# Loading the third matrices of a spare quad behind the first matrices of the quad that follows it

## The chip, the core and the metric

The kernel runs on one NeuronCore of a Trainium2 chip. The metric is the device time of one execution in microseconds (us). It computes one inference step of a two-layer backbone for 128 context tokens and 128 sample tokens with width 1024. All of its weights are float32 in HBM and are read once per execution, so the kernel moves some 290 MB.

## The reference, cut to what matters

Each of the two layers has a mixer part (modulated norm, one combined input projection, linear attention, convolution and latent attention, an output projection) and a mixture of experts. The change is in how the weights of the experts are loaded.

```python
def hier_moe(h, p):          # 32 experts in 4 groups; top 1 group, top 2 experts in it, for each token
    ...
    gate = (...)             # (tokens, 32), two entries of a row are not zero
    hid = silu(einsum('bnd,edf->bnef', h, moe_w1)) * einsum('bnd,edf->bnef', h, moe_w3)
    return einsum('bnef,efd->bnd', hid * gate[..., None], moe_w2)
# moe_w1, moe_w3: (2, 32, 1024, 256); moe_w2: (2, 32, 256, 1024): 1 MiB per expert and matrix
```

## The kernel before

**Tiles and quads.** The two routed entries of every token are put into tiles of 32 places (CAP). Each of the 32 experts has one tile of its own. An expert that more than 32 entries chose gets further tiles out of 16 spare ones. Four tiles make a quad: quads 0 to 7 are the base quads (experts 4q to 4q+3), quads 8 to 11 hold the 16 spare tiles. The order in which quads are worked on is written out by hand in ORDER (L88), `[0, 1, 8, 2, 3, 9, 4, 5, 10, 6, 11, 7]`. In what follows i is the position in this order, so the positions 2, 5, 8 and 10 are spare quads and the other eight are base quads. Which spare tiles are in use is known only at run time: SyncE reads four expert numbers with value_load (L668), and a tile that is not in use has the number 32 (NE).

**Matrices and buffers.** A quad has three matrices for each tile, of 1 MiB each. The first and second ones (moe_w1 and moe_w3) are the eight "up" matrices of a quad, and the third ones (moe_w2) its four "down" matrices. Half p=0 of a quad (tiles 0 and 1) is loaded into ring_b, half p=1 (tiles 2 and 3) into ring; in both, the slots 0 to 3 take up matrices and the slots 4 and 5 down matrices. So each half has one buffer for up matrices and one for down matrices, and there is no second buffer for the next quad. All these loads are issued by SyncE (L639 and L651) and go through one queue, q1.

**What the loads wait for.** up_weights(i, 0) waits until TensorE is done with the up matmuls of half 0 of position i-1 (L631, up_psum 2i-1). up_weights(i, 1) waits for the same of half 1 (L625 and L626). down_weights(i, 0) and (i, 1) wait until both halves of the down matmuls of i-1 are done (L643, down_psum 2i). SyncE works on its instructions in order, so an issue that waits holds every issue behind it. The order is: up 0, up 1, down 0, down 1 of i, and then those of i+1.

**Predicated loads.** The loads of a spare quad have a condition (L619): where the expert number is 32, the transfer is skipped. Its semaphore still gets its 16, and what was in the buffer stays there; the gate rows of an unused tile are zero places, so that its matmuls add nothing. TensorE works through a spare quad in full whether its tiles are used or not.

**TensorE's order** (L1420 to L1448) is also written out. For each position i: up(i) (L1394) unless i is spare; a gather of tokens for the next pair of quads (L1376); combine(i-1) (L1405), which adds the outputs of the quad before into the result; another gather; the transposes of hid (L1433); then, **if i+1 is spare, up(i+1)**; and last down(i) (L1445), which waits for the down matrices of i (L1438). So the up matmuls of a spare quad come just before the down matmuls of the quad ahead of it.

ScalarE does silu on the up results (L944) and copies hidT (L954) and y_hi (L959), VectorE forms hid (L1861) and y_lo (L1881).

Of the kernel before, what the change touches and what calls it, by code (L numbers as in the profile page):

```python
# [95 lines left out]
def spare(i):  # L96

    return i < QUADS and ORDER[i] >= BASE_QUADS
# [96 lines left out]
def build(nc, a, o):  # L195

    ctx = ExitStack()
    with ctx:
# [328 lines left out]
        def vectors(lay):  # L527

            def rows(r0, n, src):
                return vecA[r0:r0 + n, :], src.rearrange("(r p) -> r p", p=P)  # L530

            return [rows(r0, n, a[name][lay]) for r0, n, name in (
                (R_ADA, 48, "ada_b"), (R_N1, 8, "norm1_w"), (R_N2, 8, "norm2_w"), (R_GLA, 2, "gla_norm_w"), (R_CB, 2, "conv_b"),
                (R_CW, 2, "conv_ln_w"), (R_CLB, 2, "conv_ln_b"), (R_QN, 2, "mla_qnorm_w"), (R_KVN, 1, "mla_kvnorm_w"))] + [
                rows(R_FIN, 8, a["final_norm_w"]),
                (vecB[0:2 * CONV_K, :], a["conv_w"][lay].rearrange("k (t p) -> (k t) p", p=P))]
# [27 lines left out]
        def _(sp):  # L564
# [11 lines left out]
            for l in range(L):  # L576
# [37 lines left out]
                def source(name, i, x, held):  # L614

                    q = ORDER[i]
                    if q < BASE_QUADS:
                        return a[name][l, 4 * q + x], {}
                    return a[name][l, sp.snap(held[x] % NE)], {"cond": held[x] < NE}  # L619

                def ring_free(i, slot, freed):
                    if i == 0:
                        last = max(g for g in range(units(l)) if g % RING == slot)
                        sp.wait_ge(*unit_done.at(l, last + 1))
                    elif slot in (0, 4):  # L625
                        sp.wait_ge(*freed)  # L626

                def up_weights(i, p, held=None):

                    if p == 0 and i > 0:  # L630
                        sp.wait_ge(*up_psum.at(l, 2 * i - 1))  # L631
                    for g in range(4):
                        src, skip = source(("moe_w3", "moe_w1")[(g // 2) ^ p], i, 2 * p + g % 2, held)
                        if p == 0:
                            into, landed = ring_b, ring_b_up_landed
                        else:
                            ring_free(i, g, up_psum.at(l, 2 * i))
                            into, landed = ring, ring_landed[g]
                        sp.dma_start(into[:, g, :], src.rearrange("(p k) n -> p (k n)", k=KT), **skip).then_inc(landed, 16)  # L639

                def down_weights(i, p, held=None):
                    if p == 0 and i > 0:
                        sp.wait_ge(*down_psum.at(l, 2 * i))  # L643
                    for x in range(2):
                        src, skip = source("moe_w2", i, 2 * p + x, held)
                        if p == 0:
                            into, landed = ring_b, ring_b_down_landed
                        else:
                            ring_free(i, 4 + x, down_psum.at(l, 2 * i))
                            into, landed = ring, ring_landed[4 + x]  # L650
                        sp.dma_start(into[:, 4 + x, :], src.rearrange("(p k) n -> p (k n)", k=2), **skip).then_inc(landed, 16)  # L651
# [9 lines left out]
                up_weights(0, 1)  # L661
                down_weights(0, 1)
                sp.wait_ge(*eid_ready.at(l, 1))
                for i in range(1, QUADS):
                    held = None
                    if spare(i):
                        v = 4 * (ORDER[i] - BASE_QUADS)
                        held = [sp.value_load(eid[0:1, v + x:v + x + 1], min_val=0, max_val=NE) for x in range(4)]  # L668
                    up_weights(i, 0, held)
                    up_weights(i, 1, held)  # L670
                    down_weights(i, 0, held)
                    down_weights(i, 1, held)
                    if i == 1 and l + 1 < L:
                        for dst, src in vectors(l + 1):
                            sp.dma_start(dst, src).then_inc(vec_landed.sem, 16)
# [1239 lines left out]
```

## Time and profile before

| | |
|---|---|
| median of 3 runs | 1065.86 us (1064.49 to 1067.51) |
| the profiled execution, its own time | 1068.25 us |
| its span, first to last instruction | 1066.2 us |
| mean granted TensorE clock | 0.874 of full speed |
| TensorE matmul / VectorE / ScalarE busy | 796.1 (75%) / 434.5 (41%) / 260.1 us (24%) |
| queue q1 (all loads by SyncE) | 284.39 MB, 67.8% of 16 engines' span |
| SyncE's down loads waiting for TensorE's down matmuls (L651 for L1445) | 199.0 us, 22 times |
| SyncE's up loads waiting for up matmuls (L639 for L1394) | 175.6 us, 26 times |

The experts of layer 0 take about 252 to 554 us of the span, those of layer 1 about 770 to 1048 us. "DMA share" is the mean busy share of the 16 DMA engines, "PEclk" the granted clock of TensorE as a part of full speed. The duration of a load's row at SyncE is the time that its issue takes, not the transfer. A row of the timeline merges several instructions ("x4"); matmuls overlap, so the end of the last one is later than the start of the next group.

### The profile page before, as it was taken

The page shows a single profiled execution, that of the slowest core. Times are in us where ns is not written, and L with a number is a line of the kernel's source. Part 1 is how long each engine was busy: PE and PEld are TensorE (multiplying, and loading weights), DVE is VectorE, ACT ScalarE, POOL GpSimd, SP SyncE. Part 2 cuts the span into 40 slices and gives each one's busy share as a digit, 9 for nine tenths or more (in the row PEclk, how much of TensorE's full clock was granted, in tenths as well). Part 3 has the DMA queues.
Part 4 walks back from the last instruction along what each step waited for, and adds up shares of the span by engine and source line. Part 5 has one row for each costly group of instructions (what it writes and reads, how often), then busy time and mean ns, then how long its engine had stood idle before and what let it go on. Part 6 is the DMA issues. An engine that isn't in the chain of part 4 may idle for free.

```text
span 1066.2 us, 17503 instructions
## 1 busy us (share of the span) xinstructions
PE 796.1 (75%) x7505; PEld 536.6 (50%) x7505; DVE 434.5 (41%) x934; ACT 260.1 (24%) x488; POOL 36.3 (3%) x52
## 2 busy tenths in 40 slices
PE   4599899958664595687767998988668667576856
PEld 3388566835332363254345974677435334353524
DVE  1348985264211222141225798834714113122214
ACT  2356144132010110020115731533212001101103
POOL 4000100000300000000000001000000000000000
PEclk9699999968678898798888998998789889889968
DMA  9945746955949949948693486347094995977491
GB/s 339 334 140 207 288 161 234 401 238 205 408 157 424 420 178 424 420 171 342 273 367 100 159 311 245 116 179 302 10 423 187 421 381 234 421 292 313 183 424 68
DMA packets 73289, 290.51 MB, mean 272 GB/s; under 512 B 8650, under 2 KB 33948, under 8 KB 47868
## 3 DMA queue, kind: packets, MB, share of 16 engines
q1 hardware_dynamic: 69174, 284.39, 67.8%
q0 software_dynamic: 1504, 3.45, 1.0%
q10 hardware_dynamic: 2534, 1.56, 0.5%
q8 instruction: 59, 0.97, 0.4%
q14 instruction: 18, 0.15, 0.0%
HBM read 382.28 MB, written 1.47 MB: 360 GB/s over the span
## 4 chain that ended last, share of the span: by engine, by line
PE 39%; DMA 36%; DVE 13%; ACT 4%; SPq 4%; issue 2%; ACTq 0%; DVEq 0%
DMA ring<-in_moe_w 27%; PE bank L1394 13%; PE bank L1060 5%; PE bank L1445 4%; PE bank L1294 3%; DVE acc L1638 3%; SPq L639 3%; DMA ada<-in_ada_w 3%; DMA ring_b<-in_moe_w 3%; PE bank L1376 2%; DMA ring<-in_ada_w 2%; PE bank L1003 2%; PE bank L1405 1%; DMA ring<-in_w_in 1%; PE bank L1336 1%
## 5 line engine op out<-in xcount | busy, mean ns | idle before, releaser
L1861 DVE SCALAR_TENSOR_TENSOR hid<-sil,gs,bank 64x256 f32<-64x256 f32 x48 | 32.5, 676 | 323.2 <-ACT sil L944 323.2
L944 ACT ACTIVATE sil<-bank 64x256 f32<-64x256 f32 x48 | 18.1, 378 | 363.9 <-PE bank L1394 363.9
L1394 PE MATMUL bank<-ring_b,hT 128*32 128x256 f32 x768 | 60.4, 483 | 60.4 <-DMA ring_b<-in_moe_w 58.6
L1445 PE MATMUL bank<-ring_b,hidT 128*32 128x512 f32 x384 | 88.6, 603 | 12.7 <-ACT hidT L954 6.2
L1394 PE MATMUL bank<-ring,hT 128*32 128x256 f32 x768 | 60.2, 481 | 40.4 <-DMA ring<-in_moe_w 40.4
L1445 PE MATMUL bank<-ring,hidT 128*32 128x512 f32 x384 | 88.5, 603 | 0.0
L1394 PEld LDWEIGHTS bank<-ring_b,hT 128*32 128x32 f32 x768 | 31.0, 138 | 92.3 <-issue 44.0
L1394 PE MATMUL bank<-ring,xn 128*32 128x256 f32 x768 | 55.5, 452 | 28.4 <-DMA ring<-in_moe_w 28.4
L1394 PE MATMUL bank<-ring_b,xn 128*32 128x256 f32 x768 | 55.0, 450 | 26.2 <-DMA ring_b<-in_moe_w 24.7
L1394 PEld LDWEIGHTS bank<-ring,hT 128*32 128x32 f32 x768 | 34.8, 137 | 65.0 <-issue 58.2
L1638 DVE SCALAR_TENSOR_TENSOR acc<-zp,convT,acc 128x256 f32<-128x256 f32 x120 | 61.8, 556 | 1.9
L1376 PE MATMUL bank<-S,h_hi 128*128 128x256 f32 x192 | 52.7, 308 | 10.0 <-DVE y_lo L1881 8.6
L1294 PE MATMUL bank<-mixT,ring 128*128 128x256 f32 x256 | 56.9, 381 | 2.9 <-DVE mixT L1708 1.8
L1394 PEld LDWEIGHTS bank<-ring,xn 128*32 128x32 f32 x768 | 31.7, 130 | 50.9 <-issue 41.9
L1060 PE MATMUL bank<-x_hi,win_hi 128*128 128x256 f32 x192 | 55.4, 288 | 2.1 <-DVE win_lo L1534 2.1
L1394 PEld LDWEIGHTS bank<-ring_b,xn 128*32 128x32 f32 x768 | 29.7, 129 | 52.9 <-issue 27.5
L1881 DVE TENSOR_TENSOR y_lo<-bank,y_hi 128x512 fp32r<-128x512 f32 x48 | 32.8, 691 | 53.2 <-ACT y_hi L959 53.1
L1060 PE MATMUL bank<-x_lo,win_hi 128*128 128x256 f32 x192 | 54.3, 283 | 0.0
L1060 PE MATMUL bank<-x_hi,win_lo 128*128 128x256 f32 x192 | 54.3, 283 | 0.0
L1445 PEld LDWEIGHTS bank<-ring_b,hidT 128*32 128x32 f32 x384 | 23.0, 111 | 60.6 <-issue 49.0
L1294 PEld LDWEIGHTS bank<-mixT,ring 128*128 128x128 f32 x256 | 48.1, 190 | 10.5 <-DVE mixT L1708 2.6
L1376 PEld LDWEIGHTS bank<-S,h_hi 128*128 128x128 f32 x192 | 37.7, 197 | 22.7 <-DVE y_lo L1881 14.1
(342 smaller groups left out, 1471.3 us busy)
## 6 DMA issues: line engine op xcount, KB each, us to landing
ring_b<-in_moe_w SPq DMA_DIRECT2D x144, 1024.0 KB
ring<-in_moe_w SPq DMA_DIRECT2D x144, 1024.0 KB
ring<-in_ada_w SPq DMA_DIRECT2D x40, 1024.0 KB
ring<-in_w_in SPq DMA_DIRECT2D x14, 1024.0 KB
ada<-in_ada_w SPq DMA_DIRECT2D x4, 2048.0 KB, 23.7
ring<-in_w_out SPq DMA_DIRECT2D x8, 1024.0 KB
wuq<-in_mla_wuq POOLq DMA_DIRECT2D x2, 768.0 KB, 9.5
ring<-in_w_in SPq DMA_DIRECT2D x2, 640.0 KB
```

What stands on the lines that cost most here:

```text
L639: sp.dma_start(into[:, g, :], src.rearrange("(p k) n -> p (k n)", k=KT), **skip).then_inc(landed, 16)
L944: act.activation(sil[64 * p:64 * p + 64, :], B[4 + 3 * p][64 - 64 * p:128 - 64 * p, 0:256], ACT.Silu).then_inc(sil_ready.sem, 1)
L1003: ins = pe.matmul(bank[CM * t:CM * t + CM, 0:256], condS[:, k, :], w[:, k % 2, t * 256:t * 256 + 256], start=(k == 0), stop=(k == KT - 1))
L1060: ins = pe.matmul(out, weights, moving, start=(k == 0 and j == 0), stop=(k == KT - 1 and j == 2))
L1294: ins = pe.matmul(B[WOUT_BANKS[u]][:, f * T:f * T + T], w[:, k, f * P:f * P + P], mixT[:, k, :], start=(k == 4), stop=(k == 1))
L1336: ins = pe.matmul(B[5 + s][:, 0:NG + NE], hT[:, k, s * N:s * N + N], wr[:, k, :], start=(k == 0), stop=(k == KT - 1))
L1376: ins = pe.matmul(bank[:, (k % 2) * BCOLS:(k % 2) * BCOLS + BCOLS], h_part[:, s, k, :], S[:, s, :], start=(s == 0 and h_part is h_hi), sto ...
L1394: ins = pe.matmul(B[4 + 3 * p][CAP * g:CAP * g + CAP, 0:256], tokens[:, k, c:c + CAP], w[:, g, k * 256:k * 256 + 256], start=(k == 0), sto ...
L1445: ins = pe.matmul(B[5 + half][CAP * x:CAP * x + CAP, :], hidT[:, m, CAP * x:CAP * x + CAP], w[:, 4 + x % 2, m * D + half * 512:m * D + hal ...
L1638: ins = dve.scalar_tensor_tensor(acc[:, m, :, :], src, w, acc[:, m, :, :], ALU.mult, ALU.add)
L1861: dve.scalar_tensor_tensor(hid[rows_, i % 2, :].rearrange("s (m p) -> s p m", m=2), sil[rows_, :].rearrange("s (p m) -> s p m", m=2), gs[r ...
L1881: dve.tensor_tensor(y_lo[:, 512 * half:512 * half + 512], B[5 + half][:, :], y_hi[:, 512 * half:512 * half + 512].bitcast(F32), ALU.subtra ...
```

## The change

Before, SyncE issues the down loads of every position right behind its up loads. After, the down loads of a spare position i-1 are left out at i-1 and issued at the next position i, which is always a base quad (two spare quads never follow each other, and the last position is a base quad): behind up_weights(i, 0) and up_weights(i, 1), and ahead of down_weights(i, 0). Their waits and their conditions are the same, and the four register values with the expert numbers are kept for one more position (held_before). Nothing else is changed: no load is added or taken away, and the programs of the other engines are the same.

```diff
                 sp.wait_ge(*eid_ready.at(l, 1))
+                held_before = None
                 for i in range(1, QUADS):
                     held = None
                     if spare(i):
...
                     up_weights(i, 0, held)
                     up_weights(i, 1, held)
-                    down_weights(i, 0, held)
-                    down_weights(i, 1, held)
+
+                    for late in ([i - 1] if spare(i - 1) else []) + ([] if spare(i) else [i]):
+                        down_weights(late, 0, held_before if late < i else None)
+                        down_weights(late, 1, held_before if late < i else None)
+                    held_before = held
                     if i == 1 and l + 1 < L:
                         for dst, src in vectors(l + 1):
                             sp.dma_start(dst, src).then_inc(vec_landed.sem, 16)
```

| | order of SyncE's loads around a spare position 5 |
|---|---|
| before | up 5, **down 5**, up 6, down 6 |
| after | up 5, up 6, **down 5**, down 6 |

## Rows read from the trace of the kernel before

**Rows 1.** The page's chain of waits: shares of the span by engine and line.
```profile
PE 39%; DMA 36%; DVE 13%; ACT 4%; SPq 4%; issue 2%; ACTq 0%; DVEq 0%
DMA ring<-in_moe_w 27%; PE bank L1394 13%; PE bank L1060 5%; PE bank L1445 4%; PE bank L1294 3%; DVE acc L1638 3%; SPq L639 3%; DMA ada<-in_ada_w 3%; DMA ring_b<-in_moe_w 3%; PE bank L1376 2%; DMA ring<-in_ada_w 2%; PE bank L1003 2%; PE ban
```
**Rows 2.** The chain in order of time, layer 0, positions 4 to 6 (start, us, what).
```profile
349.54 22.84 DMA ring<-in_moe_w
372.62 6.03 PE bank L1394 x64
...
382.88 7.04 PE bank L1394 x128
389.92 3.48 PE bank L1445 x32
...
397.67 20.18 DMA ring<-in_moe_w
418.10 5.53 PE bank L1394 x64
```
**Rows 3.** Timeline of SyncE's queue: start, us, line, transfer, count.
```profile
393.41 0.24 SPq L651 DMA_DIRECT2D ring_b<-in_moe_w  x2
...
394.04 2.05 SPq L639 DMA_DIRECT2D ring_b<-in_moe_w  x4
...
403.20 0.81 SPq L651 DMA_DIRECT2D ring_b<-in_moe_w  x2
...
410.37 2.88 SPq L639 DMA_DIRECT2D ring_b<-in_moe_w  x4
```
**Rows 4.** Windows: busy PE, PEld, DVE, ACT, POOL; PEclk, DMA share, GB/s.
```profile
381.50:393.40 11.90, 11.85 (x172) 6.23 (x170) 4.65 (x11) 1.74 (x4) 0.00 (x0) 1.00 0.01 2
397.00:455.00 58.00, 35.69 (x382) 19.90 (x381) 12.36 (x32) 5.26 (x11) 0.00 (x0) 0.82 1.01 422
393.40:397.00 3.60, 2.21 (x18) 2.21 (x19) 0.69 (x1) 1.19 (x2) 0.00 (x0) 1.00 0.51 146
```
**Rows 5.** Timeline of TensorE, position 5: up in two halves, a gather, the first down matmuls.
```profile
382.81 3.66 PE L1394 MATMUL bank<-ring_b,xn 128*32 128x256 f32 x64
386.28 3.64 PE L1394 MATMUL bank<-ring,xn 128*32 128x256 f32 x64
...
394.79 0.39 PE L1376 MATMUL bank<-S,h_hi 128*128 128x256 f32 x1 [1.44 <-DVE y_lo L1881]
...
399.50 0.62 PE L1445 MATMUL bank<-ring_b,hidT 128*32 128x512 f32 x2 [0.47 <-ACT hidT L954]
```
**Rows 6.** DMA queues, 772 to 804 us, layer 1: packets and bytes.
```profile
DMA packets 1720, 12.53 MB, mean 391 GB/s; under 512 B 192, under 2 KB 192, under 8 KB 192
```
**Rows 7.** SyncE's skipped up loads: timeline of two groups, issue time (ns, min/median/max) of another.
```profile
789.43 0.98 SPq L639 DMA_DIRECT2D ring_b<-in_moe_w  x4
800.09 0.96 SPq L639 DMA_DIRECT2D ring<-in_moe_w  x4
```
```profile
L639 SPq DMA_DIRECT2D ring<-in_moe_w x4: 73/76/92, 283.0 to 283.8; - x4
```
**Rows 8.** The last of seven such places, layer 1, positions 10 and 11: SyncE and TensorE.
```profile
1009.94 1.92 SPq L639 DMA_DIRECT2D ring_b<-in_moe_w  x4
```
```profile
998.72 3.66 PE L1394 MATMUL bank<-ring_b,hT 128*32 128x256 f32 x64 [0.61 <-issue]
```
**Rows 9.** Layer 0, positions 2 and 3: timelines of SyncE and TensorE.
```profile
313.88 0.82 SPq L651 DMA_DIRECT2D ring_b<-in_moe_w  x2
```
```profile
300.88 6.06 PE L1394 MATMUL bank<-ring_b,hT 128*32 128x256 f32 x64 [14.06 <-DMA ring_b<-in_moe_w]
...
321.31 0.62 PE L1445 MATMUL bank<-ring_b,hidT 128*32 128x512 f32 x2 [1.75 <-issue]
```
**Rows 10.** Down matmuls behind a long idle time of TensorE, from the chain.
```profile
521.97 26.16 DMA ring<-in_moe_w
...
548.26 5.29 PE bank L1445 x32
```

## The prediction

> **What bounds the kernel now.** I read the chain of waits first, then its stretch inside the experts, then the timelines of SyncE and TensorE and the DMA shares of the same stretch. The chain's largest line is the wait for expert matrices in ring, 27% of the span, with 3% for ring_b; the up matmuls follow with 13% [rows 1]. In order of time a pattern repeats: a transfer ends, up matmuls run, and near a spare position a stretch of pure TensorE work stands in the chain, after which a transfer has to start from nothing [rows 2]. For positions 4 to 6 of layer 0, the up matrices of half 1 of position 4 arrive, TensorE does that half (6.03 us), gathers and combines, does up(5) (7.04 us, both halves) and down(4) (3.48 us), and only then does SyncE issue up(6), at 394.04 [rows 2, 3]. The DMA share shows what this costs: 0.01 from 381.5 to 393.4, then 1.01 at 422 GB/s for the next 58 us [rows 4]. So the expert part is bound by the one load queue, and it has a hole ahead of each base quad that follows a spare one. The hole is there because the order of issue puts down(5), which waits for TensorE's down(4), ahead of up(6), which waits only for up(5).
>
> **The places.** There are eight spare positions, four in each layer. The issue times tell which are empty. Two skipped down loads take 0.24 us at SyncE, two real ones 0.81 [rows 3]. At position 2 of layer 0 the first pair takes 0.82: two spare tiles are in use there [rows 9]. At the other seven positions the pairs look like the empty one. So seven places carry next to no bytes, and one carries two real third matrices.
>
> **An empty place, step by step.** Up(6), half 0, waits for up(5), half 0. Its matmuls start at 382.81 and last 3.66 us, so they end at 386.47 [rows 5]; SyncE follows 0.02 us later, at 386.49. Before, the issue was at 394.04 [rows 3]. Gain: 394.04 - 386.49 = 7.55 us. Half 1 is issued from about 389.9, when up(5) half 1 is done (386.28 + 3.64) [rows 5]; half 0 alone keeps the engines busy for 4.19 MB / 422 GB/s = 9.9 us, so that makes no hole. At the last of the seven: 1009.94 - (998.72 + 3.66 + 0.02) = 7.54 us [rows 8]. The five between give 7.54 or 7.55 in the same way.
>
> Does the whole stream move with it? Four things could be late.
>
> First, TensorE's down(5): it waits for the skipped loads, which SyncE now issues behind up(6). SyncE is done with up(6) at about 392 and waits for down(4) until 393.4 as before. The skip is over by 394, and TensorE needs it at 399.50 [rows 5], provided that a skipped load gives its 16 at once. Between 772 and 804 us the queues moved 12.53 MB, that is 12 real loads of 1.05 MB, with 192 packets under 512 B, exactly 16 for each real load [rows 6]. Eight skipped loads were issued in that stretch [rows 7] and left none. A skipped load takes 73 to 92 ns at its issue [rows 7]. So its 16 do not come through the queue, and I take them as immediate: cost 0.
>
> The Trainium skill, "DMA: Bandwidth & Descriptors", section "Why a DMA increments its semaphore by 16 and not by 1", says that engines that take no part in a transfer have their increments written by the issuing sequencer without waiting. Read for a transfer in which none takes part, this agrees with the packet count.
>
> Second, down(6): it still waits for down(5), and is issued at 403.20 [rows 3]. A transfer gets going 1.7 us behind its first issue: 146 GB/s over 3.6 us is 0.53 MB, worth 1.25 us at 422, so up(6) counts from 395.75 [rows 4]. After the change up(6) runs from 386.49 + 1.7 = 388.2 to 408.1 (8.39 MB, 19.9 us), and down(6) is ready to flow at 404.9. Spare time: 3.2 us; cost 0. If this cover went, each microsecond past it would be lost once.
>
> Third, up(7) half 0 waits for up(6) half 0 on TensorE. Its data are through at 388.2 + 9.9 = 398.1, so TensorE goes straight on from down(5), whose end released the issue at 403.20, and is done 3.66 us later, at 406.9, against an issue at 410.37 before [rows 3]; the stream needs it at 418. Fourth, everything further on is released by the landings themselves, which all move by 7.5 us. So cost 0 for both, and the next spare position starts with its whole chain moved.
>
> Seven places: 7 x 7.54 = 52.8 us.
>
> **The place with two real matrices** (layer 0, position 2). Up(3) can go at 300.88 + 6.06 + 0.02 = 306.96, where before it stood behind the down loads of 313.88 [rows 9]. But now 8.39 MB go ahead of the 2.10 MB that TensorE needs for down(2), and TensorE does down(2) before up(3). Stream: 308.7 + 10.49 MB / 422 GB/s = 333.5; landed 0.7 us later (as down(2) before: flowing from 313.88 + 1.7, 5.0 us of data, used at 321.31 [rows 9]) or up to 2.2 (as up(6), whose data were through at 415.6 and were used from 418.10 with 0.25 of that for issue [rows 2]). TensorE has then been idle for over 14 us (from 321.31 - 1.75 [rows 9]), and the down matmuls take 5.29 us as behind the long wait of [rows 10], instead of 3.48. Down(3) is issued at 339.5 to 341.0 and flows from 341.2 to 342.7. Before, the same bytes (down 2 and up 3) were through at 315.6 + 24.9 = 340.5. So the early start is given back in a new hole: a loss of 0.7 to 2.2 us. At the fast price of down it would be a gain of 0.9. I take +1.5, since the long idle time is certain, and keep -0.9 and +2.2 as ends.
>
> **The sum.** -52.8 + 1.5 = -51.3 us on the profiled execution's own 1068.25, so 1016.95. That execution is 2.39 us above the median of the runs (1065.86). Forecast: 1014.6 us. Unknown sizes of 0.5 us at each of seven places, the ends above and the 1.6 us by which runs differ give the likeliest case 1009 to 1021.
>
> **Rivals.**
> *The skipped loads wait their turn* (ends slower). Place: TensorE's wait ahead of down(5). If the 16 of a skipped load came only when all that was issued before it has landed, down(5) would wait for up(6), half 1. Its landing came 23.8 us behind the first issue (417.85 - 394.04) [rows 2, 3], now 386.49 + 23.8 = 410.3. Down(5) then takes 5.29 us at the low clock, down(6) is issued at 415.6 and flows from 417.3, against 415.6 before: 1.7 us lost at each of seven places instead of 7.5 gained. 1068.25 + 11.9 + 1.5 = 1081.7, or 1079 on the median. It decides from the point where down(5) starts later than about 408.6. The 192 packets speak against it [rows 6]; for it speaks only that no row has TensorE waiting for a skipped load with a full queue ahead. Chance 0.07.
>
> The Trainium skill, same page, section "Queues, rings and completion order", says that an engine takes its descriptors in ring order and that a semaphore's increment lands only after that engine's earlier writes. By that rule a skip that went through the rings would behave like this rival; real matrices, as those of layer 0, position 2, do by either.
>
> *The hole opens again ahead of down(6).* Gather, combine, transposes and down(5) take TensorE from 394.79 to the issue at 403.20, at full clock where the window shows it [rows 3 to 5]. If they ran at half clock, they would take up to 8.3 us more; 3.2 are covered, 5.1 lost, and 2.4 stay of each 7.5: 7 x 2.4 - 1.5 = 15.3, so 1053 us, or 1051 on the median. Against it: TensorE is not idle ahead of this stretch, before or after the change, and PEclk is 1.00 in the window [rows 4]. A smaller share of it is more likely than all. Chance 0.09.
>
> *The issue does not move*, because something else holds SyncE or the queue is already full. Against it: the queue is empty from 381.5, and SyncE's only wait there is down(4)'s. Time 1066, chance 0.04.
>
> *The forecast*: 0.80.
>
> **How the numbers follow.** About 0.3%, 3.2 us, is what a measurement of this kernel can tell from no change. Faster: 0.80 + 0.09 = 0.89. Same: 0.04. Slower: 0.07. The range starts a little under the likeliest case, at 1006, and goes up to 1038, to take in smaller shares of the second rival.
>
> **What would show it right or wrong.** Right: SyncE's first load behind each empty spare up is issued while TensorE's down matmuls of the quad ahead start, not 0.6 us behind their end; the 12 to 14 us with a DMA share near 0 shrink to about 4.5 to 6.5; no idle time of TensorE appears ahead of down at positions 5, 8 and 10; position 2 of layer 0 has a wait of some 14 us ahead of down(2) and a short hole behind it, and stands where it stood by position 4; the other stretches keep their lengths. Wrong: TensorE waits for a transfer ahead of down(5), or a hole in the DMA share between up(6) and down(6).

## The result, and the profile after

| | before | after | ratio, 95% interval |
|---|---|---|---|
| first comparison (4 runs each) | 1066.68 us median | 1025.2 us (1018.67 to 1026.62) | 0.9588 (0.9527 to 0.9649) |
| second comparison, another chip (11 and 6 runs) | 1072.75 us | 1021.97 us (1017.2 to 1026.96) | 0.9517 (0.9490 to 0.9544) |
| forecast | 1065.86 us | 1014.6 us | 0.952 |

The profiled execution after took 1026.62 us (span 1024.6 us, mean granted clock 0.879), 41.6 us less of span than the one before. The kernel moved the same 284.39 MB on q1; the share of the span rose from 67.8% to 70.7%.

SyncE's queue after, at the place of [rows 3]: start, us, line, transfer, count. L639 are up loads, L651 down loads.

```profile
390.49 2.15 SPq L639 DMA_DIRECT2D ring_b<-in_moe_w  x4
393.94 1.76 SPq L639 DMA_DIRECT2D ring<-in_moe_w  x4
397.38 0.28 SPq L651 DMA_DIRECT2D ring_b<-in_moe_w  x2
397.75 0.24 SPq L651 DMA_DIRECT2D ring<-in_moe_w  x2
407.19 0.82 SPq L651 DMA_DIRECT2D ring_b<-in_moe_w  x2
```

TensorE after, at the place of [rows 5] (the up matmuls are now L1398, the down matmuls L1449):

```profile
386.77 3.66 PE L1398 MATMUL bank<-ring_b,xn 128*32 128x256 f32 x64
390.25 3.64 PE L1398 MATMUL bank<-ring,xn 128*32 128x256 f32 x64
...
403.49 0.62 PE L1449 MATMUL bank<-ring_b,hidT 128*32 128x512 f32 x2 [0.47 <-ACT hidT L958]
...
406.94 3.64 PE L1398 MATMUL bank<-ring_b,hT 128*32 128x256 f32 x64
...
414.57 5.28 PE L1398 MATMUL bank<-ring,hT 128*32 128x256 f32 x64 [3.99 <-DMA ring<-in_moe_w]
```

Up(5) half 0 ends at 386.77 + 3.66 = 390.43, and up(6) is issued at 390.49, where before it came 7.57 us behind that point (394.04 against 386.47). The four skipped loads of down(5) go out at 397.38 to 398.0, while up(6) still flows: its half 1 lands only at about 414.2. TensorE does not wait for that. It starts down(5) at 403.49, held only by ScalarE's copy, as in [rows 5]. It then goes straight into up(6) half 0 with no idle time, at 406.94.

The DMA shares there, to set beside [rows 4] (columns as there):

```profile
384.50:391.50 7.00, 7.00 (x109) 4.99 (x111) 3.08 (x9) 0.77 (x2) 0.00 (x0) 1.00 0.14 50
390.50:394.00 3.50, 3.50 (x68) 2.04 (x64) 0.68 (x1) 0.43 (x2) 0.00 (x0) 1.00 0.68 225
394.00:409.00 15.00, 13.08 (x138) 7.14 (x134) 7.79 (x21) 3.70 (x7) 0.00 (x0) 1.00 1.02 425
394.00:451.00 57.00, 40.20 (x432) 22.74 (x425) 14.45 (x35) 7.55 (x16) 0.00 (x0) 0.88 1.01 422
```

The hole is 6.4 us long instead of 14.8 (one minus the DMA share, summed over 384 to 394 us after and over 380 to 397 us before), and the stream behind it has no second one: share 1.02 through 409, where down(6), issued at 407.19, has to take over, and 1.01 at 422 GB/s over 57 us.

Position 2 of layer 0, the one with two real third matrices, to set beside [rows 9]: SyncE first, then TensorE.

```profile
309.79 2.02 SPq L639 DMA_DIRECT2D ring_b<-in_moe_w  x4
313.24 1.76 SPq L639 DMA_DIRECT2D ring<-in_moe_w  x4
316.68 0.82 SPq L651 DMA_DIRECT2D ring_b<-in_moe_w  x2
317.59 0.26 SPq L651 DMA_DIRECT2D ring<-in_moe_w  x2
343.65 0.82 SPq L651 DMA_DIRECT2D ring_b<-in_moe_w  x2
```
```profile
337.17 1.07 PE L1449 MATMUL bank<-ring_b,hidT 128*32 128x512 f32 x2 [14.81 <-issue]
```

Down(2) waits 14.81 us, because its 2.1 MB flow behind the 8.4 MB of up(3); the profile names no releaser for this wait, and experiment 3 tests the reason. Down(3) is issued at 343.65, and from 335.5 to 345.1 the DMA share is 0.20:

```profile
335.50:345.10 9.60, 7.93 (x64) 2.78 (x68) 1.38 (x2) 1.20 (x2) 0.00 (x0) 0.62 0.20 48
```

**Step by step.** The table gives the time from the first load of one up group to that of the next, from the timelines of SyncE. A spare position lies in each of the first four steps (2, 5, 8 and 10); the last column is from the issue of up(11) to the end of down(11).

| profile | layer | up(1)→up(3) | →up(6) | →up(9) | →up(11) | →end |
|---|---|---|---|---|---|---|
| before | 0 | 63.16 | 78.93 | 75.81 | 44.43 | 39.2 |
| after | 0 | 55.47 | 80.70 | 67.67 | 37.72 | 39.4 |
| after, second profile | 0 | 55.34 | 80.87 | 67.71 | 37.49 | 39.2 |
| before | 1 | 44.87 | 74.31 | 74.90 | 45.09 | 37.4 |
| after | 1 | 37.54 | 67.08 | 68.50 | 37.87 | 42.3 |
| after, second profile | 1 | 40.41 | 67.71 | 68.73 | 37.76 | 40.0 |

Layer 0 lost 20.6 us from up(1) on, layer 1 23.2; 2.4 were added ahead of the experts of layer 0, where nothing was changed (up(1) issued at 254.32, before at 251.95). 20.6 + 23.2 - 2.4 = 41.4 of the 41.6.

A step also holds the landing of a whole quad, so it varies by more than the change does. The stretch on which the change acts is shorter: from the first load of the spare quad's half 1 (issued when TensorE is done with half 1 of the up matmuls ahead) to the first load of the next up group. At position 5 of layer 0 it was 379.03 to 394.04, 15.01 us, and is now 383.04 to 390.49, 7.45 us. At the seven empty places it took 14.93 to 15.64 us before and 7.42 to 8.18 us in the first profile after: 7.43 to 7.56 us less at each, where 7.54 or 7.55 was forecast. The second profile after gives the same range, 7.43 to 7.55.

### The profile page after: what moved, and what is told of

Its sections match the earlier page's. It is cut to its first block, busy times and chain, and to the rows that moved or that the text cites. A ratio compares the mean times of both kernels' runs of the same rounds, so it can differ in the third digit from the quotient of the medians.

```text
span 1024.6 us, 17503 instructions
## 1 busy us (share of the span) xinstructions
PE 781.9 (76%) x7505; PEld 535.3 (52%) x7505; DVE 434.4 (42%) x934; ACT 260.4 (25%) x488; POOL 36.5 (4%) x52
## 3 DMA queue, kind: packets, MB, share of 16 engines
q1 hardware_dynamic: 69174, 284.39, 70.7%
## 4 chain that ended last, share of the span: by engine, by line
PE 41%; DMA 32%; DVE 14%; ACT 5%; issue 4%; SPq 4%; ACTq 0%; DVEq 0%
DMA ring<-in_moe_w 24%; PE bank L1398 13%; PE bank L1064 6%; PE bank L1449 4%; DVE acc L1642 4%; PE bank L1298 4%; DMA ada<-in_ada_w 3%; PE bank L1380 3%; DMA ring<-in_ada_w 2%; SPq L639 2%; DMA ring_b<-in_moe_w 2%; PE bank L1409 2%; PE bank L1340 1%; PE bank L1007 1%; DMA ring<-in_w_in 1%
## 5 line engine op out<-in xcount | busy, mean ns | idle before, releaser
L1449 PE MATMUL bank<-ring_b,hidT 128*32 128x512 f32 x384 | 94.4, 636 | 30.3 <-issue 14.8
L1449 PE MATMUL bank<-ring,hidT 128*32 128x512 f32 x384 | 94.2, 636 | 0.0
L1398 PE MATMUL bank<-ring,hT 128*32 128x256 f32 x768 | 55.3, 451 | 32.7 <-DMA ring<-in_moe_w 32.7
L1398 PE MATMUL bank<-ring,xn 128*32 128x256 f32 x768 | 53.7, 441 | 29.6 <-DMA ring<-in_moe_w 29.6
L1398 PE MATMUL bank<-ring_b,hT 128*32 128x256 f32 x768 | 51.2, 426 | 30.4 <-DMA ring_b<-in_moe_w 28.6
L1449 PEld LDWEIGHTS bank<-ring_b,hidT 128*32 128x32 f32 x384 | 24.4, 116 | 82.0 <-issue 73.1
L1398 PE MATMUL bank<-ring_b,xn 128*32 128x256 f32 x768 | 48.6, 409 | 19.0 <-DMA ring_b<-in_moe_w 17.6
L1398 PEld LDWEIGHTS bank<-ring,hT 128*32 128x32 f32 x768 | 32.0, 130 | 55.0 <-issue 46.4
L1398 PEld LDWEIGHTS bank<-ring,xn 128*32 128x32 f32 x768 | 32.4, 127 | 49.7 <-issue 40.2
L1398 PEld LDWEIGHTS bank<-ring_b,hT 128*32 128x32 f32 x768 | 28.1, 122 | 55.4 <-issue 28.9
L963 ACT ACTIVATE y_hi<-bank 128x512 fp32r<-128x512 f32 x48 | 28.7, 597 | 100.4 <-PE bank L1449 100.4
```

The costliest lines, as they stand in the source:

```text
L963: act.activation(y_hi[:, 512 * half:512 * half + 512], B[5 + half][:, :], ACT.Copy).then_inc(yhi_ready.sem, 1)
L1398: ins = pe.matmul(B[4 + 3 * p][CAP * g:CAP * g + CAP, 0:256], tokens[:, k, c:c + CAP], w[:, g, k * 256:k * 256 + 256], start=(k == 0), sto ...
L1449: ins = pe.matmul(B[5 + half][CAP * x:CAP * x + CAP, :], hidT[:, m, CAP * x:CAP * x + CAP], w[:, 4 + x % 2, m * D + half * 512:m * D + hal ...
```

## The experiments

Kernels that stand together ran on one chip and share their runs of the kernel before.

**1. One place, one layer, all but one place.** All three change the same lines, with another condition. The one shown is that of only_8; only_l1 has `l == 1` in the brackets, not_first `not (l == 0 and q == 2)`. A spare position that is not late keeps the conditions of its own tiles (held).

```diff
-                    for late in ([i - 1] if spare(i - 1) else []) + ([] if spare(i) else [i]):
-                        down_weights(late, 0, held_before if late < i else None)
...
+                    def late_(q):
+                        return spare(q) and (q == 8)
+
+                    for late in ([i - 1] if late_(i - 1) else []) + ([] if late_(i) else [i]):
+                        down_weights(late, 0, held_before if late < i else held)
...
```

> The change at position 8 alone, in both layers. My theory: 2 x 7.5 = 15 us faster than before, about 1051 us, and the two holes ahead of up(9) shrink from 13 to about 6 us while the six others stay. Rival (a hole that is closed early is made up by a longer one further on): less than 8 us faster.

Measured: 1058.47 us beside 1073.82, ratio 0.9856 (0.9822 to 0.9889), 15.4 us faster. In its profile the steps to up(9) are 68.35 and 67.66 us, against 75.81 and 74.90 before; the other steps between up groups are within 1 us of before's. The gain of a place is its own and is not given back further on.

> The change in layer 1 alone. My theory (7.5 us at each of four places, additive): 1066 - 30 = 1036 us. Rival (the shortfall of 7 us in layer 1 seen in one profile is systematic): 1066 - 23 = 1043 us. From the profile: the step between the first loads of up(3), up(6), up(9) and up(11) is 7.2 to 7.6 us shorter each, and the stretch from up(11)'s issue to the end of down(11) is 37 us if the shortfall was a chance event, 42 if it is systematic.

Measured: 1045.07 us, ratio 0.9741 (0.9703 to 0.9779), 28.8 us faster, nearer to 30 than to 23. The steps of layer 1 are 39.40, 67.75, 68.68 and 37.70 us, and the last quad took 37.4 us. The steps are 5.5, 6.6, 6.2 and 7.4 us shorter than before's, so the 7.2 to 7.6 us expected of each came in one of four only.

> The change everywhere but at position 2 of layer 0, which has the order of before. My theory (there the early start is given back in a new hole, -0.9 to +2.2 us): 0 to 2 us faster than the changed kernel, about 1024 us. Rival (that place gained its 7.5 us like the others and the loss of 10 us against the forecast is elsewhere): 7 us slower, about 1032 us.

Measured: 1022.56 us, ratio 0.9525 (0.9491 to 0.9559). That is the level of the changed kernel (0.9517 on another chip), and 7 us slower is ruled out; a difference of 0 to 2 us can't be told from these two ratios. Its profile has 62.97 + 71.40 = 134.4 us from up(1) to up(6) in layer 0; the two profiles of the changed kernel have 136.2. By the traces the place costs 1.8 us, where 2 were expected at most. The step up(3)→up(6), 71.40 us against 78.93 before, holds the change at position 5 alone here: 7.53 us.

**2. That place alone.**

```diff
+                    def late_(q):
+                        return spare(q) and (l == 0 and q == 2)
...
```

> The change at position 2 of layer 0 alone, the one place with two real third matrices. My theory: no gain, a loss of about 1.6 us (so 0 to 3 us slower than before); in the trace up(3) is issued 7.7 us earlier than before and up(6) 1.8 us later, counted from the first load of up(1) and up(3). Rival: 7.5 us faster like an empty place.

Measured: 1074.35 us beside 1074.96, ratio 1.0001 (0.998 to 1.0022). No gain; the loss of about 1.6 us that was expected is within the interval, and so is none. In the trace up(3) comes at 55.22 us and up(6) 88.08 us later, 143.3 in all; before 142.1, and in the two kernels that leave the place alone 142.5 and 142.8. Here the second step is 9.2 us longer, where the first is 7.9 shorter.

**3. The third matrices between the halves of the next up matrices.**

```diff
                     up_weights(i, 0, held)
+                    if spare(i - 1):
+                        down_weights(i - 1, 0, held_before)
+                        down_weights(i - 1, 1, held_before)
                     up_weights(i, 1, held)
+                    if not spare(i):
+                        down_weights(i, 0, None)
+                        down_weights(i, 1, None)
```

> The third matrices of a spare quad are issued between the two halves of the next quad's up matrices, instead of behind both. My theory: the stream is as early as in the changed kernel at every place (first up half at the same time; the second half is held until the down matmuls ahead are done, 3.5 us later, while the first half still has 6 us of data), and at position 2 of layer 0 the two real matrices land 10 us earlier, so that down(3) is issued before up(3) has flown through: no second hole. Expected: 7.5 to 9 us faster than the changed kernel, about 1016 us beside 1025; down(2) of layer 0 waits about 5 us instead of 14.8. Rival (the early start of both halves is what pays, and the second half held for 3.5 us opens a hole): as slow as or slower than the changed kernel, by 8 x 2 to 4 us.

Measured: 1016.0 us, ratio 0.9455 (0.9422 to 0.9488), on the chip on which the kernel without the change at that one place (not_first) had 1022.56; the intervals of the two ratios do not overlap. Position 2 of layer 0 now: down(2)'s wait at TensorE, and the DMA share up to and across the issue of down(3) at 333.92.

```profile
327.64 1.07 PE L1451 MATMUL bank<-ring_b,hidT 128*32 128x512 f32 x2 [4.94 <-issue]
```
```profile
312.00:333.00 21.00, 14.62 (x126) 7.39 (x121) 5.25 (x12) 3.15 (x6) 0.00 (x0) 0.84 1.00 420
333.00:337.00 4.00, 4.00 (x72) 2.16 (x64) 0.69 (x1) 0.60 (x1) 0.00 (x0) 1.00 1.00 418
```

The wait is 4.94 us instead of 14.81, and there is no second hole. From up(1) to up(6) it is 55.22 + 72.68 = 127.9 us, 8.3 less than after the change. The steps behind it in layer 0 are 68.72 and 37.77 us, beside 68.62 and 37.78 in not_first (67.7 and 37.5 to 37.7 in the two profiles of the changed kernel), so no cost of holding the second half for 3.5 us can be seen. Once more, on a third chip:

> The third matrices between the halves of the next up matrices, once more, as the base of comparison for the kernel beside it. Expected: a ratio of 0.944 to 0.949 to before.

Measured: 1017.65 us beside 1074.96, ratio 0.947 (0.9443 to 0.9497).

**4. Real third matrices at every place**, in the three orders. In all three the condition of the spare down loads is dropped:

```diff
                         src, skip = source("moe_w2", i, 2 * p + x, held)
+                        skip = {}
```

> The order of before, with the third matrices of every spare tile loaded whether it is used or not (30 more real loads of 1.05 MB; unused tiles then have expert 0's matrix, with gates of zero). They go ahead of up(i+1), so the stream gets 31.5 MB / 422 GB/s = 74.5 us longer. Expected by both theories: 1066 + 74 = about 1140 us.

Measured: 1147.51 us beside 1072.75, 74.8 us more.

> The same extra loads in the order of the change. My theory (a real third matrix behind the next up matrices gives the early start back: up(i+1) flows first, down(i) lands 30 us behind its start, TensorE idles ahead of down(i), and a hole of 8.5 us opens ahead of down(i+1)): 8 places at +0.5 to +2 us, so 1140 + 4 to 16 = about 1150 us, not faster than the order of before. Rival (the gain is only in the early issue, whatever the bytes): 8 x 7.5 = 60 us faster than the order of before, 1080 us.

Measured: 1161.51 us, 14.0 us slower than the order of before: 1.75 on average over the eight places. The order that saves 7 us at an empty place loses time at a full one. Position 5 of layer 0 in its profile, in the chain (start, us, what; L1399 up, L1450 down):

```profile
392.68 7.04 PE bank L1399 x128
399.72 3.48 PE bank L1450 x32
...
404.93 24.98 DMA ring<-in_moe_w
430.04 6.36 PE bank L1450 x32
```
```profile
398.50:427.50 29.00, 8.90 (x90) 5.53 (x82) 6.50 (x19) 2.55 (x5) 0.00 (x0) 0.73 1.01 422
428.50:438.00 9.50, 7.96 (x68) 2.83 (x72) 1.38 (x2) 1.20 (x2) 0.00 (x0) 0.63 0.12 18
```

29 us of full stream (up 6, then down 5), TensorE idle for most of it, then down(5) at 430.04 in 6.36 us with a granted clock of 0.63 in that stretch, and a hole of 9.5 us until down(6) flows.

> The same extra loads, the third matrices between the halves of the next up matrices. My theory: down(i) lands 10 us earlier, down(i+1) is issued before the stream is empty, no second hole: 8 x 7.5 = 60 us faster than the order of before, about 1080 us. Rival (any real load ahead of TensorE's order costs as much as it brings): 1140 us or more.

Measured: 1089.47 us, 58.0 us faster than the order of before with the same bytes, 7.3 on average. In its profile up(6) is issued at 384.99 and 393.91, up(7) at 417.64 and 422.46, and the stream has no hole there (columns as in [rows 4]):

```profile
393.00:440.00 47.00, 27.97 (x276) 16.35 (x280) 11.33 (x31) 5.11 (x10) 0.00 (x0) 0.82 1.01 421
```

So a real load that is put late does not by itself cost what the early start brings. What decided here is how many bytes flow ahead of what TensorE needs next.

**5. The changed kernel again.**

> The changed kernel once more, beside the kernel before on the same chip. My theory (the 10 us missing from the forecast are partly the level of single executions): about 48 to 50 us faster than before, the step between the first loads of up(6), up(9) and up(11) in layer 1 shorter by 6.5 to 7.3 us each as in the four profiles so far, and the last quad of layer 1 between 37 and 42 us. Rival (a fixed cost of the change in the last quad): 42 us again there, and 41 us faster in all.

Measured: 1021.97 us beside 1072.75, 50.8 us faster, and 40.0 us in the last quad of layer 1. A gain of 41 us on this chip is out, and so is a fixed cost of the full 5 us in the last quad. Its steps up(3)→up(6)→up(9)→up(11) in layer 1 were 6.6, 6.2 and 7.3 us shorter, where 6.5 to 7.3 were expected.

**6. TensorE's order too.** The loads as in experiment 3; up(5) ahead of gather and combine(3):

```diff
                     if not spare(i):
                         up(i)
+                    if spare(i + 1) and (i + 1) % 2:
+                        up(i + 1)
...
-                    if spare(i + 1):
+                    if spare(i + 1) and not (i + 1) % 2:
                         up(i + 1)
```

> The loads as in the kernel beside it, and at position 5 (the only spare quad whose tokens are gathered before) TensorE does up(5) right behind up(4), ahead of gather and combine(3), 4 us earlier. What bounds is still the hole of about 6 us that is left ahead of up(6), so my theory expects 3 to 4 us for each layer, 6 to 8 us faster than the kernel beside it, and a step from up(3) to up(6) of about 63 us instead of 66.9 in layer 1. Rival (the hole's length no longer decides, but landings further on, or down(6), issued too late for the earlier stream): within 2 us of the kernel beside it.

Measured: 1012.91 us beside 1017.65 for the kernel of experiment 3 on the same chip, ratio to before 0.9436 (0.9402 to 0.947). The medians are 4.7 us apart, where 6 to 8 were expected, and the intervals of the two ratios overlap. The steps up(3)→up(6) went from 72.64 to 68.46 and from 66.87 to 62.75 us, as expected, but the steps behind them grew by 1.5 and 1.4 (68.61 to 70.13, 68.65 to 70.00). So the length of the hole still decides this step, with some of it given back in the next one; why was not looked into. It has the lowest median of the study.

## Why the prediction was right, and where it was off

**The bound and the place of the gain** were right. The one load queue bounds the experts, its hole sits ahead of the base quad behind a spare one, and at each of the seven empty places the next up group is issued 7.43 to 7.56 us sooner behind the spare one, in both profiles of the changed kernel, where 7.54 or 7.55 was forecast. The whole steps that hold one empty place and nothing else came out 6.2 to 8.1 us shorter, but for the first step of layer 1 in the second profile (4.5 us, below). Experiment 1 shows that the places add up. One sign was described wrongly: up(6) is not issued while TensorE's down(4) starts but 3.2 us ahead of it (390.49 and 393.70), since half 1 of up(5) lies between. The hole of 6.4 us is at the upper end of the 4.5 to 6.5 named.

**Skipped loads give their 16 at once** was right. Down(5) starts at 403.49 with up(6) still landing until 414.2, so the first rival (slower, 1079 us) is out. The skips are issued by 398.0 and used from 403.49, so "at once" is shown to within 5.5 us. The Trainium skill, "DMA: Bandwidth & Descriptors", section "Why a DMA increments its semaphore by 16 and not by 1", says that the issuing sequencer writes the increments of the engines that take no part. Of a skipped transfer it says nothing; read for one in which no engine takes part, it agrees with these times. For real matrices the order of issue holds: the matmuls that need down(2)'s two start 20.5 us after their issue (316.68 to 337.17), when the eight of up(3) ahead have had their 19.9 us. By the same page of the Trainium skill, section "Queues, rings and completion order", each engine takes its descriptors in ring order, and the trace agrees.

**Down(6) in time** was right, with the margin of 3.2 us that was worked out. Up(6) flows until 390.49 + 1.7 + 19.9 = 412.1, so the last moment for down(6) is 410.4, and it is issued at 407.19, 3.2 us ahead. The second rival is out: the share stays at 1.02.

**The place with real matrices** was forecast at +1.5 us and came out at +1.8 in the traces (+0.5 to +1.2 with that place alone), with the idle time (14.81 us against over 14), the slow down matmuls (6.42 us in the chain, where 5.29 was put in) and the second hole as described. Its lower end was worked out a little wrong: with down at 3.48 us the same terms give a gain of 1.1 us, not 0.9, which changes nothing in the sum. What the working missed is that this loss can be had back by a smaller hoist (experiment 3): it compared only the two orders given.

**The size.** -51.3 us was forecast, -41.5 measured first and -50.8 on a second chip; both medians, 1025.2 and 1021.97 us, lie above the 1009 to 1021 called likeliest. The term that was off in the first profile is the one that says all other stretches keep their length. Of the 10 us missing, 2.4 lie ahead of the experts, 0.5 in layer 0, and 7 in layer 1: about 2 in the four steps and 5 in the last quad (42.3 us against 37.4). The last quad's end, in the chain, after the change and in the kernel changed in layer 1 alone (L1452 are its down matmuls):

```profile
979.44 19.55 DMA ring<-in_moe_w
...
999.13 6.58 PE bank L1449 x32
```
```profile
1001.55 18.32 DMA ring<-in_moe_w
1020.01 3.67 PE bank L1452 x32
```

Both have the change at position 10, and one has the long end and the other the short one. Before had 3.67 us there too, and the kernel with the change at position 8 alone, which leaves position 10 as it was, 5.12. So slow matmuls (5.1 us and more, with a granted clock of 0.62 to 0.81 in windows of 8 to 10 us around them) occur with and without the change there. The slowest (6.58 and 6.56 us) were seen only with it, behind the longest waits (3.62 and 3.24 us). Over the profiles the last quad of layer 1 took 37.4, 38.7 and 38.9 us in three without the change at position 10 (before, experiment 1's first, experiment 2) and 37.4, 39.9, 40.0, 40.1, 40.1, 41.4 and 42.3 in seven with it. The start of down(11) alone came 33.5 to 33.7 us behind the issue of up(11) in the three, and 33.7 us in one and 34.6 to 35.8 us in six of the seven. So a cost of 1 to 2 us in this wait is likely, with slow matmuls on top of it in six of the seven; why was not settled.

The first step of layer 1 varies too (37.5 to 40.4 us), but not at the changed place. The first load of up(2)'s half 1 came 29.3 us behind up(1)'s before, and 29.5 and 32.3 us in the two profiles after; from there to up(3) it is 8.09 us in both. Why up(1) took longer was not looked into.

The level of single executions is part of this. Both profiled executions of the changed kernel (1026.62 and 1026.96 us) were the slowest of their comparison, and the only profile of the kernel before (1068.25 us) is a fast one of its kind: its runs lie between 1064.5 and 1077.1 us over the chips, and the first three, on which the forecast's median stood, were among the lowest. So the 41.6 us between the first two traces are less than what the medians of 11 and 6 runs give (50.8 us). How much of the shortfall is this level and how much a cost in layer 1 stays open. That the gain in the second comparison came within 0.5 us of the forecast is in part luck, since it holds such a shortfall too.

## What to carry to other kernels

- Where one queue feeds everything, look for instants at which its share is near zero and ask which wait stands ahead of the next issue. If the load behind that wait could go earlier, reorder the issues. Here the gain at an empty place was the distance between the two releases, and it was had at each place on its own.
- A load that was skipped could be put late for nothing here, but price the case in which it is real: it lands behind all the bytes issued ahead of it. Hoist only as much as covers the wait. Half of the next quad's up matrices (10 us of stream for a wait of 7 us) gave the same early start, and a gain of 58 us instead of a loss of 14 where the loads were real.

## What the runs showed of the hardware that was not expected

- A skipped transfer completes while real ones issued before it on the same queue are in flight. That was concluded from packet counts before (192 small packets for 12 real loads and eight skipped ones [rows 6]) and is seen directly after: skipped at 397.38 to 398.0, the matmuls that need it running at 403.49, the 8 MiB ahead landed at 414.2.
- The 32 down matmuls of a quad took 3.47 to 3.69 us where TensorE had kept working and 4.97 to 6.58 behind most waits for a landing, with a granted clock of 0.62 and 0.63 in two such stretches. At the last quad of layer 1, 1.05 and 1.77 us of idle time were followed by 3.67 us at a granted clock of 1.00, and 2.27 to 3.62 us by 5.1 to 6.6 us with 0.62 to 0.81 in the windows around them (one matmul about 1.06 us instead of 0.59).
